# The first modulation slabs shared between VectorE and TensorE, the gain and bias steps spread out, and the last unit split by tile

## The chip, the cores and the metric

The kernel runs on one core of a Trainium2 chip. The metric is the device time of one execution in microseconds, and of the times of several executions the median. The core has TensorE (matrix products into PSUM), VectorE, ScalarE and GpSimd, and SyncE, which only issues DMAs. Each engine works off its own instructions in program order and meets the others at semaphores.

## What is computed

Two layers of a decoder trunk, 256 tokens by 2048 features in float32. Each layer has a mixer (8 attention heads and 8 short-convolution groups, one input and one output projection) and an MLP, and each of the two is modulated by a vector that comes from the condition c.

```python
cond = jax.nn.silu(c)
for l in range(DEPTH):
    mod = cond @ w_mod[l] + b_mod[l]
    sh1, sc1, g1, sh2, sc2, g2 = jnp.split(mod[:, None, :], 6, axis=-1)
    u = x * (1.0 + sc1) + sh1
    proj = u @ w_in[l]
    ...                                   # attention and convolution -> mixed
    x = _layer_norm(DEEPNORM_ALPHA * x + (1.0 + g1) * (mixed @ w_out[l]), ln1_g[l], ln1_b[l])
    u = x * (1.0 + sc2) + sh2
    ff = jnp.square(jax.nn.relu(u @ w_ff1[l])) @ w_ff2[l]
    x = _layer_norm(DEEPNORM_ALPHA * x + (1.0 + g2) * ff, ln2_g[l], ln2_b[l])
```

## The kernel before

**Products.** Every large product is split into high and low parts: an activation is `hi` + `lo`, a weight is `w_hi` + `w_lo`, and three products of 128x512 (L1249 to L1251, in `half` L1263 to L1265) stand for one. The work is cut into *units* (one block of 512 output columns, 16 chunks of the inner dimension) and a unit into 8 *groups* of two chunks: 12 matmuls each, six for either tile of 128 tokens. A layer has 16 mixer units and 32 MLP units. A group's weights (512 KB) come by a DMA from SyncE into one of 4 `raw` buffers. ScalarE copies them to `w_hi` (L455), VectorE makes `w_lo` = raw - w_hi (L755), four groups ahead of their use. A position `p` = 8u + j is group j of unit u, and every engine does its side work of a position beside that group (`side`). The order is written out by hand, through tables of positions.

**Modulation.** `w_mod` is cut into 24 slabs of 1024 columns, and a slab into 16 chunks of 128x1024 (512 KB each). VectorE forms `mod_acc` = sum of chunk k times cond[k] (L766 for the first chunk, L770 for the others, one instruction each). Then TensorE sums `mod_acc` over the partitions with eight 128x1 products against ones (L1325; each shows as two records, so a sum is x16), and VectorE adds the bias. GpSimd issues the chunks' DMAs when a buffer is free.

**The head.** The first four slabs (`START_SLABS`) hold the shift and scale of the first mixer. Slab q gives what four chunks of x need, so the first three units (24 groups) run in four *quarters* of six groups: `start_fill(q)` turns x (L1350, four transposes, twice) and sums slab q between the two; ScalarE applies scale and shift; VectorE makes the low part; six groups follow, and VectorE works on slab q+1 meanwhile. `start_raw` holds 8 chunks. SyncE first loads nine small tensors with one semaphore (`small_in`, the condition is the eighth), and all engines wait for all nine.

**Fills.** Between two sub-layers, x is normalised and turned again (`last_unit`, then `first_unit`). There are three such *fills*. In `first_unit` ScalarE applies scale and shift to each turned tile (L496, four pieces), makes the high part (L500), and VectorE the low part (L828). VectorE's `gain` then multiplies x by the layer norm's g and adds b (L877, L880, two instructions each) for four column blocks, in groups 4 to 7 of that unit. The next step of VectorE in the second layer is the rotary step (`rotate`, L1083 on) at position 7, for the turned q at `Q_AT` = 10.

**The last unit** before a fill does its first four groups for both tiles, then the halves for tile 0 of groups 4 to 7, then the halves for tile 1, so that tile 0 can be finished early. The sum of slab 9 stands among those halves (position 124) in the first mixer. At the very end ScalarE normalises four blocks for each tile, and VectorE's `gain` multiplies and adds for each block.

## Time and profile before

| | |
|---|---|
| median of 3 runs | 2389.97 us (2387.24 to 2394.49) |
| the profiled execution | 2390.11 us |
| its span, first to last instruction | 2388.4 us |
| TensorE busy | 2270.1 us (95%) |
| VectorE busy | 1728.5 us (72%) |
| ScalarE busy | 1115.9 us (47%) |
| chain that ended last | TensorE 84%, VectorE 8%, DMA 3%, issue 3%, ScalarE 2% |
| mean granted clock of TensorE | 0.983 |

The time outside the span is 1.7 us. The page's part 5 groups instructions by line: busy time, mean of one, and the idle time before them with what ended it. A busy TensorE overstates its work where matmuls overlap, so starts of successive matmuls are read from the timeline instead. Where the trace has no clock record (before the first one), the column prints 1.00.

### The profile page before, as it was taken

Reading aid. Unit: us, or ns where it says so; the run is one execution under the profiler, and the core shown is the slowest. Engines: PE = TensorE matmul, PEld = TensorE weight load, DVE = VectorE, ACT = ScalarE, POOL = GpSimd, SP = SyncE. Lnnn points to the kernel's source line nnn. Section 1 sums busy time; section 2 is a strip of 40 time slices with the busy share of each in tenths; the row PEclk is TensorE's granted clock in tenths of the full one; section 3 lists DMA queues with packets and bytes.
Section 4 is the critical chain, followed back from the end, with each engine's and each line's share of the span. In section 5 each row is a group of like instructions: output and inputs, shape, how many; then the busy total and the mean of one; then the engine's idle time right before and its main releaser. Section 6 shows DMA issues by size and latency. Waiting matters only on the chain.

```text
span 2388.4 us, 30251 instructions
## 1 busy us (share of the span) xinstructions
PE 2270.1 (95%) x10384; PEld 1881.5 (79%) x10384; DVE 1728.5 (72%) x1913; ACT 1115.9 (47%) x1424; POOL 227.3 (10%) x400
## 2 busy tenths in 40 slices
PE   3689999989999999999998999999999999999997
PEld 2577888778888888888877888887888888888885
DVE  6898888868777767667878877877766555555566
ACT  2235543356435435435454554435643543543543
POOL 2211111110101101000010100101000000000000
PEclk9789999989999999999999999999999999999998
DMA  9987988958888888887965777886677666666563
GB/s 354 390 289 283 306 324 316 325 211 283 285 283 293 287 276 298 276 276 268 321 242 184 267 262 257 287 293 220 224 237 242 206 213 215 213 205 193 177 228 123
DMA packets 174733, 623.14 MB, mean 261 GB/s; under 512 B 19728, under 2 KB 20496, under 8 KB 174096
## 3 DMA queue, kind: packets, MB, share of 16 engines
q1 hardware_dynamic: 114128, 407.50, 49.8%
q0 software_dynamic: 55296, 201.35, 24.8%
...
## 4 chain that ended last, share of the span: by engine, by line
PE 84%; DVE 8%; DMA 3%; issue 3%; ACT 2%; ACTq 0%; SPq 0%; DVEq 0%; POOLq 0%
PE bank L1249 25%; PE bank L1251 25%; PE bank L1250 25%; DVE mod_acc L770 3%; PE bank L1350 2%; PE bank L1325 2%; DVE w_lo L755 1%; DMA raw<-w_out_dram 1%; DMA Z<-w_mod_dram 1%; ACT w_hi L455 1%; PE bank L1263 1%; PE bank L1264 1%; PE bank L1265 1%; ACT utmp L496 0%; DVE xt L877 0%
## 5 line engine op out<-in xcount | busy, mean ns | idle before, releaser
L755 DVE TENSOR_TENSOR w_lo<-raw,w_hi 128x1024 fp32r<-128x1024 f32 x768 | 937.8, 1224 | 563.7 <-ACT w_hi L455 561.7
L455 ACT ACTIVATE w_hi<-raw 128x1024 fp32r<-128x1024 f32 x768 | 812.4, 1059 | 1129.2 <-PE bank L1251 988.4
L1249 PE MATMUL bank<-w_hi,u_hi 128*128 128x512 f32 x1744 | 695.3, 399 | 0.3 <-DVE u_lo L813 0.3
L1251 PE MATMUL bank<-w_lo,u_hi 128*128 128x512 f32 x1744 | 682.0, 391 | 0.0
L1250 PE MATMUL bank<-w_hi,u_lo 128*128 128x512 f32 x1744 | 681.5, 391 | 0.0
L1249 PE MATMUL bank<-w_hi,m_hi 128*128 128x512 f32 x1216 | 476.9, 392 | 2.8 <-DVE m_lo L813 2.6
L1251 PE MATMUL bank<-w_lo,m_hi 128*128 128x512 f32 x1216 | 474.5, 390 | 0.0
L1250 PE MATMUL bank<-w_hi,m_lo 128*128 128x512 f32 x1216 | 474.3, 390 | 0.0
L770 DVE SCALAR_TENSOR_TENSOR mod_acc<-mod_raw,cond,mod_acc 128x1024 f32<-128x1024 f32 x300 | 383.7, 1279 | 0.6 <-DMA mod_raw<-w_mod_dram 0.6
L1251 PEld LDWEIGHTS bank<-w_lo,u_hi 128*128 128x128 f32 x1744 | 328.9, 189 | 70.0
L1249 PEld LDWEIGHTS bank<-w_hi,u_hi 128*128 128x128 f32 x1744 | 329.5, 189 | 68.6 <-issue 1.4
L1250 PEld LDWEIGHTS bank<-w_hi,u_lo 128*128 128x128 f32 x1744 | 329.5, 189 | 67.3 <-issue 1.4
L435 POOL DMA_DIRECT2D mod_raw<-w_mod_dram x316 | 167.0, 528 | 1745.6 <-DVE mod_acc L770 1521.0
L1249 PEld LDWEIGHTS bank<-w_hi,m_hi 128*128 128x128 f32 x1216 | 229.1, 188 | 51.3 <-DVE m_lo L813 3.4
L1251 PEld LDWEIGHTS bank<-w_lo,m_hi 128*128 128x128 f32 x1216 | 228.9, 188 | 48.0
L1250 PEld LDWEIGHTS bank<-w_hi,m_lo 128*128 128x128 f32 x1216 | 229.0, 188 | 47.0 <-issue 0.2
L1325 PE MATMUL bank<-ones,mod_acc 128*128 128x1 f32 x256 | 38.1, 279 | 50.2 <-DVE mod_acc L770 50.2
L770 DVE SCALAR_TENSOR_TENSOR mod_acc<-Z,cond,mod_acc 128x1024 f32<-128x1024 f32 x60 | 76.9, 1282 | 6.0 <-DMA Z<-w_mod_dram 2.3
L1325 PEld LDWEIGHTS bank<-ones,mod_acc 128*128 128x128 f32 x256 | 38.7, 235 | 52.8 <-issue 30.3
L1350 PE MATMUL bank<-idn,Z 128*128 128x128 f32 x416 | 55.0, 276 | 6.6 <-DVE gate L808 5.4
L1350 PEld LDWEIGHTS bank<-idn,Z 128*128 128x128 f32 x416 | 49.0, 142 | 14.2 <-issue 6.1
L813 DVE TENSOR_TENSOR m_lo<-utmp,m_hi 128x512 fp32r<-128x512 f32 x72 | 49.4, 692 | 14.6 <-ACT m_hi L479 14.6
(128 smaller groups left out, 1116.5 us busy)
## 6 DMA issues: line engine op xcount, KB each, us to landing
raw<-w_ff_dram SPq DMA_DIRECT2D x512, 512.0 KB, 4.2
...
```

Source lines behind the costliest of these rows:

```text
L435: pool.dma_start(mod_raw[:, k:k + 1, :], chunk(r * MODS + (first + k))).then_inc(mod_in[k], 16)
L455: nc.scalar.activation(w_hi[:, j % AHEAD, :], raw[:, j % RAW, :], ACT.Copy).then_inc(hi_ready, 1)
L755: nc.vector.tensor_tensor(w_lo[:, j % AHEAD, :], raw[:, j % RAW, :], w_hi[:, j % AHEAD, :].bitcast(F32), ALU.subtract).then_inc(lo_ready, 1)
L770: ins = nc.vector.scalar_tensor_tensor(out=a, in0=src, scalar=cond[:, k:k + 1], in1=a, op0=ALU.mult, op1=ALU.add)
L813: nc.vector.tensor_tensor(lo[:, chunk:chunk + 2, :], src, hi[:, chunk:chunk + 2, :].bitcast(F32), ALU.subtract).then_inc(split_ready, 1)
L1249: nc.tensor.matmul(o, hi[:, k, tok], wh, start=(k == 0), stop=False)
L1250: nc.tensor.matmul(o, lo[:, k, tok], wh, start=False, stop=False)
L1251: ins = nc.tensor.matmul(o, hi[:, k, tok], wl, start=False, stop=(k == KC - 1))
L1263: nc.tensor.matmul(o[:], hi[:, k, tok], wh, start=(k == 0), stop=False)
L1264: nc.tensor.matmul(o[:], lo[:, k, tok], wh, start=False, stop=False)
L1325: ins = nc.tensor.matmul(b[:, c:c + 1], mod_acc[:, par, c * P:(c + 1) * P], ones[:, 0:1], start=True, stop=True)
L1350: ins = nc.tensor.transpose(b[:, c * SEQ + t * P:c * SEQ + (t + 1) * P], src(c, t), idn[:])
```

## The change

- **Condition first.** SyncE loads c, then the identity and the modulation bias, then the first part of x, then the six other small tensors. The semaphores are separate, so the first steps wait for c alone.
- **Odd chunks on TensorE.** In the four head slabs VectorE multiplies the even chunks only. TensorE multiplies each odd chunk itself (`start_chunk`: eight 128x1 products with the chunk as the stationary operand), accumulating in PSUM bank 5, and the slab's sum is added into the same bank. Bank 4 serves the head's transposes. For slab 0 all eight odd chunks stand ahead of the first turn; for slabs 1 to 3 two chunks stand behind each of the first four groups of the quarter.
- **Gain and bias steps.** They leave groups 4 to 7 of `first_unit` for positions 9, 11, 13, 17 (mixer; MLP: 9, 12, 14, 17). In the second layer `Q_AT` goes from 10 to 14, and waits are added on ScalarE where a buffer is shared with g and b. The modulation chunks of positions 8 to 15 go to later ones.
- **Fills.** VectorE applies scale and shift to two of four pieces of tiles 4 to 7 (`affine`); ScalarE waits for that and does the other two. In `last_unit` the side work of group 7 moves behind tile 1's first half, VectorE finishes tile 0 first, and slab 9's sum goes there, to position 127.
- **The very last unit** runs all eight groups for tile 0, then all for tile 1. Its first four groups' weights lie in `u_hi` and `u_lo`. VectorE alone normalises with two instructions for each block (`centre`, `scaled`).

```diff
-Q_AT = [[22, 34], [10, 34]]
+Q_AT = [[22, 34], [14, 34]]
...
-RED_NOT_BEFORE = {16: MIXER_AT[1] + 8, 17: MIXER_AT[1] + 12}
+RED_NOT_BEFORE = {9: MIXER_AT[0] + 8 * U_MIX - 1, 16: MIXER_AT[1] + 8, 17: MIXER_AT[1] + 12}
...
+GAIN_ORDER = {1: (0, 1, 2, 3), 2: (2, 0, 1, 3), 3: (0, 1, 2, 3)}
+MIX_GAIN_AT = (9, 11, 13, 17)
+FF_GAIN_AT = (8 + 1, 8 + 4, 8 + 6, 16 + 1)
...
-                    + [8 * u + 1 for u in (1, 2, 3, 4, 9, 10, 11, 12, 13)])
+    mixer1 = sorted([8 * u + j for u in range(2, 15) for j in (0, 2, 4, 6)]
+                    + [8 * u + 1 for u in range(2, 14)])
+    ff1 = sorted([8 * w + 4 for w in range(3, 25)] + [8 * w + 1 for w in range(3, 13)])
...
+        def weights(w, ex, unit, j):
+            if unit == FINAL and j < EARLY:
+                return ex[:].rearrange("p k n -> p (k n)")[:, j * GW:(j + 1) * GW]
+            return w[:, j % AHEAD, :]
...
-            small = [(idn[:], ident), (cs[:], cos), (sn[:], sin), (msk[:], mask), (mod_b[:], b_mod),
-                     (mixg[:], mix_g), (cw[:], conv_w), (cc_in[:], cond_c), (lnc[:], ln_cols)]
-            for dst, src in small:
-                sp.dma_start(dst, src).then_inc(small_in, 16)
+            sp.dma_start(cc_in[:], cond_c).then_inc(c_in, 16)
+            sp.dma_start(idn[:], ident).then_inc(first_in, 16)
+            sp.dma_start(mod_b[:], b_mod).then_inc(first_in, 16)
...
             load_x(0)
+            small = [(cs[:], cos), (sn[:], sin), (msk[:], mask), (mixg[:], mix_g), (cw[:], conv_w), (lnc[:], ln_cols)]
+            for dst, src in small:
+                sp.dma_start(dst, src).then_inc(small_in, 16)
...
-                    pool.wait_ge(mod_used, 8 * r + (k - 7))
+                    if k % 2:
+                        pool.wait_ge(chunk_used, 4 * r + ((k - 1) // 2 - 3))
+                    else:
+                        pool.wait_ge(mod_used, 4 * r + (k // 2 - 3))
...
-                    act.wait_ge(pair_used, 8 * unit + (j - AHEAD + 1))
-                nc.scalar.activation(w_hi[:, j % AHEAD, :], raw[:, j % RAW, :], ACT.Copy).then_inc(hi_ready, 1)
+                    act.wait_ge(pair_used, 8 * unit + (j - AHEAD + 1 if unit < FINAL or j < EARLY else j - GROUPS + 1))
+                nc.scalar.activation(weights(w_hi, u_hi, unit, j), raw[:, j % RAW, :], ACT.Copy).then_inc(hi_ready, 1)
...
+                act.wait_ge(turn_done, i + 1)
+                if i >= 2:
+                    act.wait_ge(split_ready, i - 1)
+                for c in range(2):
+                    k = 2 * i + c
+                    ins = nc.scalar.activation(utmp[:, i % 2, c * SEQ:(c + 1) * SEQ], tb[0][:, c * SEQ:(c + 1) * SEQ],
+                                               ACT.Identity, bias=u_shift[:, k:k + 1], scale=u_scale[:, k:k + 1])
+                ins.then_inc(turn_read, 1)
+                act.wait_ge(turn_read, i + 1)
+                nc.scalar.activation(u_hi[:, 2 * i:2 * i + 2, :], utmp[:, i % 2, :], ACT.Copy).then_inc(split_hi, 1)
...
+                if i >= 4:
+                    act.wait_ge(aff_ready, 4 * (fill - 1) + i - 3)
+                for c in range(4 if i < 4 else 2):
...
-            act.wait_ge(small_in, 16 * 9)
+            act.wait_ge(c_in, 16)
             act.wait_ge(ones_ready, 3)
             nc.scalar.activation(cc_e[:], cc_in[:], ACT.Exp, scale=-1.0).then_inc(cond_exp, 1)
+            prepare(0, 0, first=True)
+            prepare(0, 1, first=True)
+            start_fill(0)
+            prepare(0, 2, first=True)
+            prepare(0, 3, first=True)
+            act.wait_ge(small_in, 16 * 6)
...
-                for s in range(4):
-                    normalise(fill, t, s)
...
+            def affine(fill, i):
+                t, s = NORM_ORDER[i]
+                job, n = JOB[("fill", fill)] + i, fill_split(fill, i)
+                wait_job(dve, job)
+                dve.wait_ge(split_ready, n - 1)
+                for c in range(2, 4):
+                    k = 4 * s + c
+                    ins = nc.vector.tensor_scalar(utmp[:, n % 2, c * P:(c + 1) * P], tb[job % 2][:, c * P:(c + 1) * P],
+                                                  u_scale[:, k:k + 1], u_shift[:, k:k + 1], ALU.mult, ALU.add)
+                ins.then_inc(aff_ready, 1)
...
+            def centre(t):
+                for s in range(4):
+                    dve.wait_ge(gb_in[s], 32 * 2 * DEPTH)
+                    sl = xt[:, t, s * NCOL:(s + 1) * NCOL]
+                    nc.vector.scalar_tensor_tensor(out=sl, in0=sl, scalar=mv[:, t, 0:1], in1=lngb[:, s, 0, :],
+                                                   op0=ALU.subtract, op1=ALU.mult)
+            def scaled(t):
+                for s in range(4):
+                    sl = xt[:, t, s * NCOL:(s + 1) * NCOL]
+                    nc.vector.scalar_tensor_tensor(out=sl, in0=sl, scalar=rst[:, t:t + 1], in1=lngb[:, s, 1, :],
+                                                   op0=ALU.mult, op1=ALU.add).then_inc(x_ready, 1)
...
-                for j in range(EARLY, GROUPS):
+                for j in range(EARLY, GROUPS - 1):
                     side(j)
+                last_tile(fill, unit, alpha, 0)
+                side(GROUPS - 1)
                 modulation(fill)
-                last_tile(fill, unit, alpha, 0)
...
+                    if j < 4:
+                        affine(fill, 4 + j)
                     ahead(unit, j)
...
-                        gain(fill, j - 4)
...
+            def start_mod(n, i):
+                k = 2 * i
+                q = n * KC + k
+                mod_step(n, k, n % 2, start_raw[:, q % 8, :], start_in[q % 8], (q // 2, 16 * (q // 8 + 1)))
...
-                one(0)
+                        mod_next(2 * i)
+                        mod_next(2 * i + 1)
                 start_scale(q)
-                one(1)
+                some(0)
                 start_low(2 * q)
-                one(2)
+                some(1)
                 start_low(2 * q + 1)
-                one(3)
...
+                    if layer and p in MIX_GAIN_AT:
+                        gain(2 * layer, MIX_GAIN_AT.index(p))
...
-                                if i < 4:
-                                    start_mods(q + 1, 4 + 3 * i, 3)
+                                start_mod(q + 1, 2 + i)
...
-            start_mods(0, 0, KC)
+            for i in range(KC // 2):
+                start_mod(0, i)
+            dve.wait_ge(first_in, 16 * 2)
...
-            fill, unit = 2 * DEPTH, DEPTH * U_LAYER - 1
-            last_tile(fill, unit, 1.0, 0)
-            last_root(fill, 0)
-            gain(fill, 0, (0,))
-            last_tile(fill, unit, 1.0, 1)
-            gain(fill, 1, (0,))
-            last_root(fill, 1)
-            gain(fill, 2, (0,))
-            gain(fill, 3, (0,))
-            for s in range(4):
-                gain(fill, s, (1,))
+            for t in range(T):
+                last_tile(2 * DEPTH, FINAL, 1.0, t)
+                centre(t)
+                sync(root(norm_index(2 * DEPTH, t), slice(t, t + 1)))
+                scaled(t)
...
+                both = 0 if unit == FINAL else EARLY
+                for j in range(both):
                     group(8 * unit + j, j % AHEAD, GK * j, pacc[par], hi, lo)
                     side(j)
-                for j in range(EARLY, GROUPS):
-                    ins = half(8 * unit + j, j % AHEAD, GK * j, pacc[par][0], 0, hi, lo)
+                for j in range(both, GROUPS):
+                    ins = half(unit, j, pacc[par][0], 0, hi, lo)
                     if j == GROUPS - 1:
                         ins.then_inc(half_done, 1)
-                    side(j)
-                for j in range(EARLY, GROUPS):
-                    half(8 * unit + j, j % AHEAD, GK * j, pacc[par][1], 1, hi, lo).then_inc(pair_used, 1)
+                    else:
+                        side(j)
+                for j in range(both, GROUPS):
+                    half(unit, j, pacc[par][1], 1, hi, lo).then_inc(pair_used, 1)
+                    if j == EARLY:
+                        side(GROUPS - 1)
...
+            def start_chunk(n, i):
+                k = 2 * i + 1
+                q = n * KC + k
+                if n == 0 and i == 0:
+                    pe.wait_ge(cond_ready, 1)
+                if n and i == 0:
+                    pe.wait_ge(sum_read, n)
+                pe.wait_ge(start_in[q % 8], 16 * (q // 8 + 1))
+                for c in range(SC):
+                    ins = nc.tensor.matmul(tb[1][:, c:c + 1], start_raw[:, q % 8, c * P:(c + 1) * P], cond[:, k:k + 1],
+                                           start=(i == 0 and c == 0), stop=False)
+                ins.then_inc(chunk_used, 1)
+            def start_sum(n):
+                pe.wait_ge(mod_used, KC // 2 * (n + 1))
+                for c in range(SC):
+                    ins = nc.tensor.matmul(tb[1][:, c:c + 1], mod_acc[:, n % 2, c * P:(c + 1) * P], ones[:, 0:1],
+                                           start=False, stop=(c == SC - 1))
+                ins.then_inc(sum_done, 1)
...
+                start_turn(2 * q)
+                start_sum(q)
+                start_turn(2 * q + 1)
             def start_units(side):
+                for i in range(KC // 2):
+                    start_chunk(0, i)
...
+                    if q + 1 < START_SLABS and i < START_LABELS - 2:
+                        start_chunk(q + 1, 2 * i)
+                        start_chunk(q + 1, 2 * i + 1)
                     if q + 1 < START_SLABS and i == START_LABELS - 2:
                         start_fill(q + 1)
+                pe.wait_ge(turn_read, 2 * START_SLABS)
+                pe.wait_ge(sum_read, START_SLABS)
```

**TensorE in the head.** Before, from the start of the program; L1350 turns x, L1325 is the sum, L1249 to L1251 the products:

```order
L1350 MATMUL bank<-idn,xt 128x128 x4
L1325 MATMUL bank<-ones,mod_acc 128x1 x8
L1350 MATMUL bank<-idn,xt 128x128 x4
L1249 MATMUL bank<-w_hi,u_hi 128x512
L1250 MATMUL bank<-w_hi,u_lo 128x512
L1251 MATMUL bank<-w_lo,u_hi 128x512
```

After, the same place (L1430 is an odd chunk's product with cond, L1448 the turn, L1438 the sum):

```order
L1430 MATMUL bank<-cond,Z 128x1 x64
L1448 MATMUL bank<-idn,xt 128x128 x4
L1438 MATMUL bank<-ones,mod_acc 128x1 x8
L1448 MATMUL bank<-idn,xt 128x128 x4
L1311 MATMUL bank<-w_hi,u_hi 128x512
L1312 MATMUL bank<-w_hi,u_lo 128x512
L1313 MATMUL bank<-w_lo,u_hi 128x512
```

Sixty-four 128x1 products, eight odd chunks, now stand ahead of the first turn. And after, at the end of the first group and the start of the second, where before the products follow on one another:

```order
L1311 MATMUL bank<-w_hi,u_hi 128x512
L1312 MATMUL bank<-w_hi,u_lo 128x512
L1313 MATMUL bank<-w_lo,u_hi 128x512
L1430 MATMUL bank<-cond,Z 128x1 x16
L1311 MATMUL bank<-w_hi,u_hi 128x512
L1312 MATMUL bank<-w_hi,u_lo 128x512
L1313 MATMUL bank<-w_lo,u_hi 128x512
```

Two chunks (x16) stand between two groups.

**VectorE in the head**, second quarter. Before (L770 a chunk, L755 the low part of weights):

```order
L755 TENSOR_TENSOR w_lo<-raw,w_hi 128x1024 x2
L770 SCALAR_TENSOR_TENSOR mod_acc<-Z,cond,mod_acc 128x1024 x3
L755 TENSOR_TENSOR w_lo<-raw,w_hi 128x1024
L770 SCALAR_TENSOR_TENSOR mod_acc<-Z,cond,mod_acc 128x1024 x3
L755 TENSOR_TENSOR w_lo<-raw,w_hi 128x1024
L770 SCALAR_TENSOR_TENSOR mod_acc<-Z,cond,mod_acc 128x1024 x3
L755 TENSOR_TENSOR w_lo<-raw,w_hi 128x1024
L770 SCALAR_TENSOR_TENSOR mod_acc<-Z,cond,mod_acc 128x1024 x3
```

After (L802 a chunk, L787 the low part):

```order
L787 TENSOR_TENSOR w_lo<-raw,w_hi 128x1024 x2
L802 SCALAR_TENSOR_TENSOR mod_acc<-Z,cond,mod_acc 128x1024
L787 TENSOR_TENSOR w_lo<-raw,w_hi 128x1024
L802 SCALAR_TENSOR_TENSOR mod_acc<-Z,cond,mod_acc 128x1024
L787 TENSOR_TENSOR w_lo<-raw,w_hi 128x1024
L802 SCALAR_TENSOR_TENSOR mod_acc<-Z,cond,mod_acc 128x1024
L787 TENSOR_TENSOR w_lo<-raw,w_hi 128x1024
L802 SCALAR_TENSOR_TENSOR mod_acc<-Z,cond,mod_acc 128x1024
```

One chunk stands where three did.

**VectorE in the first unit of the second layer.** Before (L877 and L880 gain and bias, L1083 the rotary step):

```order
L755 TENSOR_TENSOR w_lo<-raw,w_hi 128x1024
L877 TENSOR_TENSOR xt<-xt,Z 128x512 x2
L880 TENSOR_TENSOR xt<-xt,Z 128x512 x2
L755 TENSOR_TENSOR w_lo<-raw,w_hi 128x1024
L877 TENSOR_TENSOR xt<-xt,Z 128x512 x2
L880 TENSOR_TENSOR xt<-xt,Z 128x512 x2
L1083 TENSOR_TENSOR Z<-bank,cs 128x4x64 x2
```

After (L921 and L924 gain and bias, L1148 to L1159 the rotary step):

```order
L787 TENSOR_TENSOR w_lo<-raw,w_hi 128x1024 x4
L1148 TENSOR_TENSOR Z<-bank,cs 128x4x64 x2
L1149 TENSOR_TENSOR Z<-bank,nsn 128x4x64
L1150 TENSOR_TENSOR Z<-bank,sn 128x4x64
L1159 TENSOR_TENSOR Z<-Z 128x512
L1148 TENSOR_TENSOR Z<-bank,cs 128x4x64 x2
L1149 TENSOR_TENSOR Z<-bank,nsn 128x4x64
```

The rotary step no longer has the gains ahead of it; they come behind it.

## Rows read from the trace of the kernel before

**Rows 1.** Stretches of the head; columns: busy of each engine, clock, DMA share, GB/s.
```profile
0.00:46.50 46.50, 5.78 (x25) 4.92 (x25) 26.02 (x31) 7.81 (x11) 13.99 (x30) 1.00 0.90 340
46.50:78.00 31.50, 20.20 (x85) 17.25 (x86) 28.79 (x28) 8.37 (x11) 8.32 (x16) 0.81 1.03 407
```

**Rows 2.** Timeline of the opening: start us, us, engine, line, work, [idle before <-releaser].
```profile
15.32 0.22 ACT L729 ACTIVATE cc_e<-cc_in 128x16 f32<-128x16 f32 x1 [12.89 <-DMA lnc<-ln_cols_dram]
...
17.43 16.57 DVE L770 SCALAR_TENSOR_TENSOR mod_acc<-Z,cond,mod_acc 128x1024 f32<-128x1024 f32 x12
...
17.53 1.09 PE L1350 MATMUL bank<-idn,xt 128*128 128x128 f32 x4 [17.53 <-DMA xt<-x_dram]
...
39.94 3.58 PE L1325 MATMUL bank<-ones,mod_acc 128*128 128x1 f32 x16 [21.32 <-DVE mod_acc L770]
...
46.50 0.80 PE L1249 MATMUL bank<-w_hi,u_hi 128*128 128x512 f32 x1 [0.28 <-DVE u_lo L813]
```

**Rows 3.** Timeline of TensorE in the second quarter, and where the last begins.
```profile
71.73 3.55 PE L1325 MATMUL bank<-ones,mod_acc 128*128 128x1 f32 x16 [9.71 <-DVE mod_acc L770]
...
86.93 0.39 PE L1249 MATMUL bank<-w_hi,u_hi 128*128 128x512 f32 x1
...
89.65 0.39 PE L1249 MATMUL bank<-w_hi,u_hi 128*128 128x512 f32 x1
...
142.25 0.78 PE L1249 MATMUL bank<-w_hi,u_hi 128*128 128x512 f32 x1
```

**Rows 4.** Timeline of TensorE around a slab sum in a dense stretch.
```profile
316.14 1.84 PE L1325 MATMUL bank<-ones,mod_acc 128*128 128x1 f32 x16
317.84 0.49 PE L1249 MATMUL bank<-w_hi,u_hi 128*128 128x512 f32 x1
```

**Rows 5.** Stretches by granted clock, columns as in rows 1.
```profile
103.50:107.10 3.60, 3.55 (x16) 3.47 (x16) 2.80 (x4) 0.00 (x0) 0.68 (x2) 0.50 1.02 409
407.50:414.20 6.70, 6.70 (x21) 5.54 (x21) 5.45 (x9) 0.94 (x2) 1.05 (x2) 0.50 0.76 276
404.10:407.40 3.30, 2.16 (x15) 1.62 (x14) 1.09 (x2) 2.12 (x3) 0.53 (x1) 1.00 1.01 402
489.40:499.60 10.20, 9.49 (x30) 8.20 (x31) 2.30 (x6) 0.00 (x0) 0.53 (x1) 0.50 0.77 262
509.90:513.20 3.30, 3.30 (x9) 2.57 (x8) 3.23 (x7) 2.96 (x5) 2.72 (x1) 0.50 0.50 144
1238.20:1257.00 18.80, 13.95 (x74) 10.75 (x73) 13.43 (x22) 16.53 (x36) 6.88 (x4) 1.00 0.56 196
1284.70:1288.10 3.40, 3.02 (x12) 2.77 (x13) 3.40 (x5) 1.20 (x2) 0.11 (x1) 0.50 0.67 170
```

**Rows 6.** Timeline of TensorE, last unit of the first mixer and fill 1.
```profile
490.11 3.54 PE L1325 MATMUL bank<-ones,mod_acc 128*128 128x1 f32 x16 [2.87 <-DVE mod_acc L770]
...
509.63 0.56 PE L1263 MATMUL bank<-w_hi,u_hi 128*128 128x512 f32 x1 [2.60 <-issue]
```

**Rows 7.** Timeline of TensorE, first unit of the second layer (fill 2).
```profile
1253.68 0.63 PE L1382 MATMUL bank<-idn,xt 128*128 128x128 f32 x4 [0.86 <-ACT utmp L496]
...
1256.69 0.63 PE L1382 MATMUL bank<-idn,xt 128*128 128x128 f32 x4 [0.99 <-ACT utmp L496]
...
1285.08 1.94 PE L1350 MATMUL bank<-idn,Z 128*128 128x128 f32 x8 [5.44 <-DVE gate L808]
```

**Rows 8.** Timeline of the tail, TensorE's last product, then VectorE.
```profile
2370.91 0.39 PE L1265 MATMUL bank<-w_lo,m_hi 128*128 128x512 f32 x1
```

**Rows 9.** Timeline of the tail, VectorE.
```profile
2355.84 2.36 DVE L755 TENSOR_TENSOR w_lo<-raw,w_hi 128x1024 fp32r<-128x1024 f32 x2
...
2372.03 0.69 DVE L892 TENSOR_TENSOR bank<-bank,gate 128x512 f32<-128x512 f32 x1
...
2374.50 0.15 DVE L902 TENSOR_SCALAR ve<-mv 128x1 f32<-128x1 f32 x1
...
2384.14 0.69 DVE L880 TENSOR_TENSOR xt<-xt,Z 128x512 f32<-128x512 f32 x1
```

121 lines of the change are left out of this document (60 added, 61 removed).

## The prediction

> **What bounds the kernel now.** The table first: TensorE is busy in 95% of the span and holds 84% of the chain that ended last. So the questions are where TensorE waits, where it runs at half clock, and what the change adds to it. The stretches and TensorE's timeline answer them. In the opening nothing starts until the small tensors are in: ScalarE's first step comes at 15.3, VectorE then multiplies chunks at 1.38 us each, the first slab sum starts at 39.94 and the first product at 46.50 [rows 2]. In the second quarter TensorE idles 9.7 us for VectorE's chunks, sums slab 1 at half clock (3.55 us), and the last quarter's first products start at 142.25 [rows 3]. From 46.50 to 142.25 are 95.75 us, three quarters of 31.9 us. That looks like a VectorE bound, but the DMA column stands at 1.03 with 407 GB/s [rows 1]. A quarter needs 16 chunks, six groups of weights and a part of x, 23 x 0.524 MB = 12.1 MB, and that takes 29.6 us at this rate. A quarter can gain 2.3 us at most, whatever VectorE does.
>
> **The opening.** With c loaded first, the wait of 12.89 us [rows 2] goes, and data is late next. The first odd chunk is the second of 512 KB. At 340 GB/s [rows 1], with x between and some 3 us until the first bytes, I put it at 7.4 us (bounds 5 and 10). Eight odd chunks on TensorE cost what a slab sum costs, since shape, type and count are the same (eight 128x1 products, x16 records): 3.58 us in this part of the program [rows 2]. 7.4 + 8 x 3.58 = 36.0. VectorE's eight even chunks take 8 x 1.38 = 11 us and hide. Then the turn, 1.1 us, which before was done early (at 17.53) and now stands behind the chunks, the sum, 3.6, and the way from the sum's end to the first product, 46.50 - 43.52 = 3.0 [rows 2]. The first product starts at **43.7** against 46.5. If TensorE took the chunks at full clock the data would set the pace: 16 chunks, four weights and a part of x are 11 MB, 30 us, and the first product comes at 38.
>
> **The three quarters.** VectorE loses 8 x 1.38 = 11 us a quarter, and TensorE gets eight chunks. A group is 89.65 - 86.93 = 2.72 us [rows 3]. A sum in a dense stretch costs 1.70 us from its start to the next product's start, and 0.14 more in the first product behind it, 1.84 in all [rows 4]; so a pair of chunks costs 1.84 + 1.70 = 3.54. The turns and the sum between groups: 1.84 plus the 3.0 from above, 4.8. At full clock a quarter is 6 x 2.72 + 4 x 3.54 + 4.8 = 16.3 + 14.2 + 4.8 = **35.3 us**, over the 31.9 of before and over the 29.6 of the DMA. The idle time that VectorE caused is filled with more work than it was long. This is the bound from below: 3 x 35.3 = 105.9, 10.2 us more than before.
>
> Now the clock. What holds it up? In 103.50:107.10 TensorE is busy 3.55 of 3.60 us with nothing but 128x1 products, and the clock is 0.50 and stays there until wide products have run [rows 5]. In 404.10:407.40 it is busy 2.16 of 3.30 us, about half of that in 128x1 products, and from 407.50 on the clock is 0.50 for 6.7 us [rows 5]. In 1238.20:1257.00 it is idle for a quarter of the time but works in wide products and turns, and keeps 1.00 [rows 5]. In these rows 128x1 products did not hold the clock up. The new quarter has four stretches of 3.5 us and one of 4.8 us without a wide product. Stretches of that length without one, behind work at full clock, are few: in 404.10:407.40 and on, and at the starts of the fills, where two turns and the wait for the first tile make 3.6 us. The clock fell in the first, and at fill 1 (509.90), but not at fill 2 (1238.20) [rows 5, 6]. A single sum of 1.8 us in dense work never lowered it. I take four falls a quarter. A fall lasts 3.3 us (509.90), 6.7 us (407.50) or 10.2 us (489.40) [rows 5], and half of it is lost, 1.7 to 5.1 us. I take 2.5, between the first two, because every pair of chunks is followed by a group of wide products that can raise the clock again: 10 us a quarter. Ends of the range: nothing, and half clock throughout, where a quarter doubles to about 68 us. So a quarter is 45.3 us, three are 135.9, and the last quarter's products start at 43.7 + 135.9 = 179.6 against 142.25: **+37.4 us**. TensorE is the bound behind it, so nothing of this is given back.
>
> The Trainium skill, "TensorE: Matmul & The Clock Gate", section "Why this matters for your kernels", tells to avoid idle gaps between bursts of matmuls and to keep TensorE busy continuously, and gives idle time as what lowers the clock. By that advice the chunks in the old 9.7 us gap are good for the clock, and the result is the second case below. The row of 103.50:107.10 does not agree: busy, and at 0.50.
>
> **The sum of slab 9.** TensorE waits 2.87 us for VectorE at 490.11 [rows 6] and then runs 10.2 us at 0.50 [rows 5], 5.1 lost. It is moved three halves of tile 0 and one of tile 1 later, 4 x 1.36 = 5.4 us, more than the wait. VectorE's chunks before it stay. The fill's scale needs the sum, but tile 0's mean and variance are being made at that time. **-8.0 us** (0 to -8).
>
> **Gain and bias, and q.** TensorE waits 5.44 us for q at 1285.08 [rows 7], and the clock is 0.50 for 3.4 us behind it [rows 5]. VectorE had four gains ahead of the rotary step, each four instructions of 0.69 that overlap a little [rows 9], 2.6 us. Now the step stands ahead of them and q is turned four positions later, 11 us. The wait and 1.7 us of half clock go: **-7.1 us** (0 to -7.1). The moved gains and chunks lie in units in which VectorE has 2.72 us a group for 1.2 (low part) and at most one 1.3 or 2.6; I cost them at nothing. If that cover is missing, they show as waits for `w_lo`.
>
> **Fills.** TensorE waits 0.86 and 0.99 us for ScalarE's four pieces [rows 7], three fills, 5.6 us in all. Half of the pieces go to VectorE, but ScalarE waits for them, one more hand-over each. I take **-3 us** (-5.6 to +2). The 2.60 us wait at 509.63 [rows 6] is one tile's way through three engines with all four pieces still on ScalarE, and stays.
>
> **Tail.** The last product starts at 2370.91 [rows 8], and the end is at 2388.4. The last unit starts 96 x 0.2265 = 21.7 us earlier, at 2349.4. With halves first, group 4's low weights are needed 4 x 1.36 us later, at 2354.8, but VectorE makes them behind the last residual, from 2355.84 on, and one takes half of 2.36 [rows 9]: 2357.0: TensorE waits **+2.2 us**. Tile 0 is finished and stored under tile 1's products. Tile 1 needs, after its last product, at 2373.5: the step from L892 to L902, 2374.65 - 2372.03 = 2.6; four `centre` at some 0.65 = 2.6; the root, five steps as small as L902, at 0.2 = 1.0; four `scaled` 2.6; and the last store as before, 2388.4 - 2384.83 = 3.6 [rows 9]. 2373.5 + 12.4 = 2385.9, **-2.5 us** in all.
>
> **Sum.** Against the profiled execution, 2390.11 (span 2388.4 and 1.7 around it; the median of the runs is 2389.97, so one stands for the other): +37.4 - 8.0 - 7.1 - 3 - 2.5 = +16.8, **2406.9 us**.
>
> **The rivals.** Second case, not slower: *the chunk products keep the clock that wide products raised*. It decides at 1.00 in the quarters. The opening stays at 43.7, the quarters take 105.9, products of the last start at 149.6, +7.3; with -20.6 from the rest, 2376.8. For it: at 1238.2 a stretch as long did not lower the clock. Against: the two rows of 128x1 work. Chance 0.18. With the opening at full clock as well, 2371, 0.04. Third: *falls are shorter or rarer*, 5 us a quarter in place of 10: 2391.9, chance 0.12. Fourth: *the savings do not come*, because VectorE's moved gains, the hand-over in the fills and the last unit's low weights only change which wait is last (the -7.1, -3 and -2.5 gone): 2419.5, chance 0.12. Fifth: *half clock throughout the quarters*: 43.7 + 3 x 68 = 248, +105 - 20.6 = 2475, chance 0.04; the group of 5.1 us at half clock between two pairs speaks against it, as wide products of 5 to 7 us raised the clock each time. My forecast has 0.50.
>
> **How the numbers follow.** About 0.3% (7.2 us) can be told from no change here. Faster (under 2382.8): second case, 0.22. Same: third case and the edge of the forecast, 0.15. Slower: the rest, 0.63. The range leaves out the fifth case, the full opening and some of the edges: 2374 to 2424. The forecast's own range is 2396 to 2418.
>
> **What would show it.** The new line of 128x1 products with 3.5 us for two at 0.50 and 1.8 and 1.7 at 1.00; first wide product near 43.7; TensorE without idle in the quarters and VectorE idle for some 11 us in each; clock under 0.8 from 44 to 180; the last quarter's products at 180. No wait at slab 9's sum nor at the turn of q; a wait of 2 us for low weights in the last unit. If the last quarter's products start before 150, the clock step is wrong; if a chunk costs under 1.2 us, the price from the sum's row is.

## The result and the profile after

The changed kernel takes 2430.52 us (median of 4 runs, 2428.29 to 2433.19) against 2390.91: ratio 1.0167, 95% interval 1.015 to 1.0184. The profiled execution is the one of 2428.29 us, with a span of 2426.6. I had forecast 2406.9 and a range of 2374 to 2424: slower was right, the size was not, +38.2 us in the span where I had +16.8.

The busy line, the line of the clock (40 slices; a 9 is 0.9 or more) and the group of the new 128x1 products, from the page after:

```profile
PE 2364.4 (97%) x10896; PEld 1969.8 (81%) x10896; DVE 1695.3 (70%) x1903; ACT 1101.5 (45%) x1392; POOL 227.3 (9%) x400
PEclk9678999999999999999999999999999999999998
L1430 PE MATMUL bank<-cond,Z 128*128 128x1 f32 x512 | 77.3, 285 | 11.1 <-DMA Z<-w_mod_dram 11.1
```

TensorE is busier than before (97%), and the kernel is slower. The 32 chunks cost it 77.3 us of busy time, and the clock is below 0.9 in slices 2 to 4. The stretches of the opening, of the three quarters and of what follows answer to [rows 1, 5]. The columns are the stretch and its length in us, the busy time and count of TensorE's products, its weight loads, VectorE, ScalarE and GpSimd, then the granted clock, the DMA share and GB/s:

```profile
0.00:46.20 46.20, 33.21 (x153) 32.49 (x153) 14.56 (x22) 5.52 (x8) 13.48 (x29) 1.00 0.97 372
46.20:93.40 47.20, 42.39 (x213) 37.69 (x213) 18.59 (x20) 10.42 (x14) 8.44 (x16) 0.75 0.78 283
93.40:143.50 50.10, 45.29 (x226) 39.38 (x225) 18.12 (x20) 9.64 (x12) 8.44 (x16) 0.74 0.64 221
143.50:195.80 52.30, 47.49 (x227) 41.65 (x225) 19.21 (x20) 9.64 (x12) 6.30 (x12) 0.70 0.52 190
195.80:540.00 344.20, 337.48 (x1593) 279.77 (x1592) 302.70 (x380) 157.84 (x239) 49.08 (x93) 0.99 0.88 310
```

A quarter takes 47 to 52 us in place of 31.9. The DMA, which bounded it before (1.03), falls to 0.52, so it is TensorE that bounds it now. (The 1.00 of the first row is no sign of full clock: the products in it take 3.5 us, as at 0.50. The column has no record there.) ScalarE's first step and TensorE's timeline at the marks (start us, us, what, count, idle before it and what ended it):

```profile
2.67 0.21 ACT L760 ACTIVATE cc_e<-cc_in 128x16 f32<-128x16 f32 x1 [0.23 <-DMA cc_in<-c_dram]
7.55 3.54 PE L1430 MATMUL bank<-cond,Z 128*128 128x1 f32 x16 [7.55 <-DMA Z<-w_mod_dram]
30.94 3.57 PE L1430 MATMUL bank<-cond,Z 128*128 128x1 f32 x16 [2.07 <-DMA Z<-w_mod_dram]
46.18 0.79 PE L1311 MATMUL bank<-w_hi,u_hi 128*128 128x512 f32 x1 [0.27 <-DVE u_lo L845]
87.46 3.57 PE L1438 MATMUL bank<-ones,mod_acc 128*128 128x1 f32 x16 [3.22 <-DVE mod_acc L802]
195.77 0.78 PE L1311 MATMUL bank<-w_hi,u_hi 128*128 128x512 f32 x1
546.55 1.84 PE L1391 MATMUL bank<-ones,mod_acc 128*128 128x1 f32 x16
571.51 0.63 PE L1486 MATMUL bank<-idn,xt 128*128 128x128 f32 x4 [0.93 <-ACT utmp L522]
2397.04 0.53 PE L1325 MATMUL bank<-w_hi,m_hi 128*128 128x512 f32 x1 [2.14 <-DVE w_lo L787]
2414.90 0.39 PE L1327 MATMUL bank<-w_lo,m_hi 128*128 128x512 f32 x1
```

The opening gained almost nothing (46.18 against 46.50). The last quarter's products start at 195.77 against 142.25 [rows 3], +53.5 us. Slab 9's sum (546.55) has no wait, where it had one of 2.87 [rows 6]. The last product starts at 2414.90 against 2370.91 [rows 8], +44.0. So the savings behind the quarters came, and the quarters ate them.

An idle time that I had not foreseen stands before the sum at 87.46 (3.22 us), and again at 139.23 and 189.84. VectorE's timeline just ahead of it:

```profile
84.98 1.23 DVE L787 TENSOR_TENSOR w_lo<-raw,w_hi 128x1024 fp32r<-128x1024 f32 x1 [7.10 <-ACT w_hi L472]
86.12 1.28 DVE L802 SCALAR_TENSOR_TENSOR mod_acc<-Z,cond,mod_acc 128x1024 f32<-128x1024 f32 x1
91.06 0.17 DVE L1007 TENSOR_TENSOR mod_col<-bank,mod_b 128x8 f32<-128x8 f32 x1 [3.66 <-PE bank L1438]
```

VectorE has 7 us to spare and its last chunk is there to take. But in its program the step stands behind a low part of weights. That waits for `w_hi`, and ScalarE makes `w_hi` only when TensorE is through with the group that used the same buffer (83.89, 8.47 us idle for it), which is the last one ahead of the sum. So the last chunk step can't begin before the quarter's products are done, and the sum waits for it.

### The profile page after: what moved, and what is told of

Read it like the earlier page. It is cut to its first block, busy times and chain, and to the rows that moved or that the text cites. A ratio compares the mean times of both kernels' runs of the same rounds, so it can differ in the third digit from the quotient of the medians.

```text
span 2426.6 us, 31262 instructions
## 1 busy us (share of the span) xinstructions
PE 2364.4 (97%) x10896; PEld 1969.8 (81%) x10896; DVE 1695.3 (70%) x1903; ACT 1101.5 (45%) x1392; POOL 227.3 (9%) x400
## 4 chain that ended last, share of the span: by engine, by line
PE 92%; DVE 4%; issue 1%; DMA 1%; ACT 1%; ACTq 0%; POOL 0%; DVEq 0%; POOLq 0%; SPq 0%
PE bank L1311 27%; PE bank L1313 27%; PE bank L1312 27%; PE bank L1430 3%; PE bank L1416 2%; PE bank L1325 1%; PE bank L1326 1%; PE bank L1327 1%; DVE mod_acc L802 1%; DMA Z<-w_mod_dram 1%; PE bank L1391 1%; ACT w_hi L472 1%; DVE w_lo L787 1%; PE bank L1438 1%; PE bank L1400 0%
## 5 line engine op out<-in xcount | busy, mean ns | idle before, releaser
L787 DVE TENSOR_TENSOR w_lo<-raw,w_hi 128x1024 fp32r<-128x1024 f32 x764 | 933.2, 1224 | 624.9 <-ACT w_hi L472 622.6
L1311 PE MATMUL bank<-w_hi,u_hi 128*128 128x512 f32 x1744 | 705.9, 405 | 0.3 <-DVE u_lo L845 0.3
L1313 PE MATMUL bank<-w_lo,u_hi 128*128 128x512 f32 x1744 | 690.3, 396 | 0.0
L1312 PE MATMUL bank<-w_hi,u_lo 128*128 128x512 f32 x1744 | 690.2, 396 | 0.0
L1313 PE MATMUL bank<-w_lo,m_hi 128*128 128x512 f32 x1200 | 468.7, 391 | 0.0
L1312 PE MATMUL bank<-w_hi,m_lo 128*128 128x512 f32 x1200 | 468.5, 390 | 0.0
L1311 PEld LDWEIGHTS bank<-w_hi,u_hi 128*128 128x128 f32 x1744 | 335.2, 192 | 69.3 <-issue 1.4
L1312 PEld LDWEIGHTS bank<-w_hi,u_lo 128*128 128x128 f32 x1744 | 335.1, 192 | 68.8 <-issue 1.4
L802 DVE SCALAR_TENSOR_TENSOR mod_acc<-mod_raw,cond,mod_acc 128x1024 f32<-128x1024 f32 x300 | 383.6, 1279 | 0.2
L1312 PEld LDWEIGHTS bank<-w_hi,m_lo 128*128 128x128 f32 x1200 | 226.3, 189 | 46.5 <-issue 0.2
L1430 PEld LDWEIGHTS bank<-cond,Z 128*128 128x128 f32 x512 | 78.7, 243 | 12.7 <-issue 7.5
L1430 PE MATMUL bank<-cond,Z 128*128 128x1 f32 x512 | 77.3, 285 | 11.1 <-DMA Z<-w_mod_dram 11.1
L1416 PE MATMUL bank<-idn,Z 128*128 128x128 f32 x416 | 54.1, 273 | 1.2 <-DVE Z L1159 1.1
L802 DVE SCALAR_TENSOR_TENSOR mod_acc<-Z,cond,mod_acc 128x1024 f32<-128x1024 f32 x28 | 35.8, 1280 | 19.6 <-DMA Z<-w_mod_dram 19.6
```

The source lines that it names most:

```text
L787: nc.vector.tensor_tensor(weights(w_lo, u_lo, unit, j), raw[:, j % RAW, :], weights(w_hi, u_hi, unit, j).bitcast(F32), ALU.subtract).then_ ...
L802: ins = nc.vector.scalar_tensor_tensor(out=a, in0=src, scalar=cond[:, k:k + 1], in1=a, op0=ALU.mult, op1=ALU.add)
L1311: nc.tensor.matmul(o, hi[:, k, tok], wh, start=(k == 0), stop=False)
L1312: nc.tensor.matmul(o, lo[:, k, tok], wh, start=False, stop=False)
L1313: ins = nc.tensor.matmul(o, hi[:, k, tok], wl, start=False, stop=(k == KC - 1))
L1416: ins = nc.tensor.transpose(b[:, c * SEQ + t * P:c * SEQ + (t + 1) * P], src(c, t), idn[:])
```

## The experiments

The theory from here on: the rest of the change is a gain, and the chunk products on TensorE cost some 59 us, by their own time at full clock (14 us a quarter), by half clock that comes with 3.5 us stretches without a wide product, and by VectorE's order ahead of the sums. The rivals: the rest of the change costs too; TensorE's share of narrow work lowers the clock, however it is spread; the chunks' waits and hand-overs cost the time, not the products. All runs are set against runs of the kernel before on the same chip (medians 2388.6 to 2390.8).

**All chunks back on VectorE.**

```diff
-START_SHARE = START_SLABS * KC // 2
+START_SHARE = START_SLABS * KC
 def start_mod(n, i):
-    k = 2 * i
+    k = i
 ...
-    start_chunk(q + 1, 2 * i)
-    start_chunk(q + 1, 2 * i + 1)
```

> The changed kernel with all 64 chunks of the head back on VectorE in the old order; condition first, gains, fills and last unit stay as changed. Theory A (the chunk products on TensorE are the whole loss, the rest of the change is a gain): the opening is paced by data, 16 chunks, and the first product comes near 38; the quarters take 31.9 us as before, so the last quarter's products start near 134, 62 us ahead of the changed kernel's 195.8: about 2367 us. Rival B (the rest of the change costs too, or the head's new banks and waits do): the last quarter's products start later than 140 or the end lies above 2385.

Measured: 2371.42 us (2369.07 to 2372.81), ratio 0.9916 (0.9899 to 0.9932). That is 59 us under the changed kernel and 19 under the one before. Its sums and first products, from TensorE's timeline:

```profile
36.10 3.57 PE L1440 MATMUL bank<-ones,mod_acc 128*128 128x1 f32 x16 [24.48 <-DVE mod_acc L799]
42.66 0.80 PE L1311 MATMUL bank<-w_hi,u_hi 128*128 128x512 f32 x1 [0.28 <-DVE u_lo L842]
133.15 3.54 PE L1440 MATMUL bank<-ones,mod_acc 128*128 128x1 f32 x16 [7.82 <-DVE mod_acc L799]
139.05 0.77 PE L1311 MATMUL bank<-w_hi,u_hi 128*128 128x512 f32 x1
```

Two of its quarters, from the view of stretches:

```profile
42.70:74.60 31.90, 20.15 (x85) 17.16 (x86) 28.91 (x29) 10.57 (x15) 8.48 (x16) 0.80 1.03 408
74.60:107.10 32.50, 23.14 (x97) 19.35 (x95) 27.48 (x28) 9.54 (x12) 8.01 (x16) 0.76 1.00 387
```

The clock is hardly higher here (0.80, 0.76) than in the changed kernel. But TensorE is idle for a third of the quarter, and the data sets the pace (1.03, 1.00), so little hangs on it. The head without TensorE's chunks, with the condition loaded first, brings the first product 3.8 us forward (42.66 against 46.50), not the 8.5 us that I had expected: VectorE waits for the data of most chunks, and starts on the last one at 34.76. The run ends 4 us later than the 2367 of theory A for that reason. The rest of the change is a gain, as forecast.

**VectorE's chunk steps earlier in the quarter.** Two steps in the first group of a quarter and one in each of the next, so that none is left for the last.

```diff
-start_mod(q + 1, 2 + i)
+for s in ((2, 3), (4,), (5,), (6,), (7,), ())[i]:
+    start_mod(q + 1, s)
```

> The changed kernel with VectorE's last even chunk of each slab one group earlier, ahead of the low part that waits for the group just run. Theory A (the 3.4 us idle before the sums of slabs 1 to 3 is this order on VectorE): the idle goes, 10 us, and up to 5 us of half clock with it: 2413 to 2421 us. Rival B (the sum waits for data, or the idle only stands in for something as late): 2428 to 2431 us, the idle stays with another releaser.

Measured: 2417.26 us (2414.06 to 2418.61), ratio 1.0109 (1.0092 to 1.0126), 13 us under the changed kernel, as expected. TensorE's timeline at the sum and the first product of the next quarter:

```profile
83.31 1.84 PE L1439 MATMUL bank<-ones,mod_acc 128*128 128x1 f32 x16
87.68 0.78 PE L1312 MATMUL bank<-w_hi,u_hi 128*128 128x512 f32 x1
```

Its three quarters, from the view of stretches:

```profile
45.70:87.70 42.00, 40.20 (x213) 35.70 (x213) 18.76 (x20) 10.49 (x14) 8.44 (x16) 0.77 0.86 318
87.70:135.10 47.40, 45.65 (x227) 39.97 (x225) 18.09 (x20) 9.65 (x12) 8.44 (x16) 0.72 0.68 244
135.10:182.60 47.50, 45.75 (x226) 39.84 (x225) 19.03 (x20) 9.65 (x12) 6.30 (x12) 0.72 0.55 198
```

The idle time before the sum is gone, and the sum, in dense work now, runs at full clock (1.84 for 3.57). It was VectorE's order that made it. The quarters are 42.0, 47.4 and 47.5 us, 45.6 in the mean.

**The same chunks, spread.** As the last run, but of the two chunks behind a group one is moved into the middle of the group, so that no stretch without a wide product is longer than 1.7 us, the quarter's turn and sum aside. Same work, same share.

```diff
 for kk in range(GK):
+    if kk == 1 and mid is not None:
+        mid()                        # start_chunk(q + 1, 2 * i)
     k = k0 + kk
```

> The second kernel of this set (last chunk early) with the same eight chunks a slab on TensorE, but one in the middle of each of the four groups and one behind it, so no stretch without a wide product is over 1.8 us, except at the turns. Theory A (the length of the stretches lowers the clock): the clock holds 1.00 but for the turns, a quarter takes 36 to 39 us in place of 46 to 47, about 2385 to 2395 us. Rival B (the share of 128x1 work counts, whatever its pieces): the same time as the second kernel within 5 us.

Measured: 2387.52 us (2383.21 to 2395.96, 10 runs), ratio 0.9991 (0.9977 to 1.0004), 30 us under the last run. A chunk in its timeline, 1.84 us between wide products:

```profile
51.87 1.84 PE L1433 MATMUL bank<-cond,Z 128*128 128x1 f32 x16
```

Its three quarters, and a stretch behind a turn:

```profile
45.70:80.30 34.60, 32.84 (x213) 29.62 (x213) 18.69 (x20) 10.43 (x14) 8.40 (x16) 0.99 0.97 372
80.30:117.00 36.70, 34.95 (x227) 31.44 (x225) 18.11 (x19) 9.45 (x12) 8.16 (x17) 0.96 0.84 316
117.00:153.90 36.90, 35.15 (x226) 31.54 (x224) 18.78 (x20) 9.59 (x13) 6.23 (x13) 0.95 0.71 266
...
80.30:83.10 2.80, 2.80 (x9) 2.22 (x8) 2.53 (x3) 1.65 (x3) 0.04 (x1) 0.50 0.90 351
```

The clock falls only at the turns, 3.4 us each time, and a quarter is 36.1 us in the mean. Set the two runs side by side: the clock lacks 0.23, 0.28 and 0.28 of the three quarters there, 9.7 + 13.3 + 13.3 = 36 us, and 0.3 + 1.5 + 1.8 = 4 us here; the quarters differ by 136.9 - 108.3 = 28.6 us, so the clock accounts for all of it and comes out some 4 us high. In the code nothing but the order of TensorE's products differs. So it is the arrangement that lowers the clock here, and the rival by share falls.

**A quarter of the chunks on TensorE.** From the changed kernel: only every fourth chunk goes to TensorE, one behind a group; VectorE takes 12 of 16.

```diff
-    k = 2 * i + 1
+    k = 4 * i + 3
 ...
-    start_chunk(q + 1, 2 * i)
-    start_chunk(q + 1, 2 * i + 1)
+    start_chunk(q + 1, i)
```

> The changed kernel with only every fourth chunk on TensorE (four a slab, one behind each of the first four groups), twelve on VectorE, all of them ahead of the group's wait. Theory A: TensorE has 16.3 + 4 x 1.84 + 4.8 = 28.5 us a quarter at full clock, VectorE 12 x 1.38 + 7.3 + 2 = 26, the DMA 29.6, so a quarter takes 30 to 31.5 us at the DMA's pace, the clock stays high, the first product comes near 38 and the last quarter's near 131: 2360 to 2367 us. Rival B (VectorE's chain of chunk, low part and sum binds all the same, or the clock falls in single chunks too): a quarter of 33 us or more, over 2372 us.

Measured: 2386.64 us (2381.15 to 2390.09, 10 runs), ratio 0.9978 (0.9966 to 0.9989). Theory A was 20 us too low, and the numbers are those of rival B: quarters of 34.4, 37.8 and 38.4 us. The first product stands at 45.66, not near 38, since the opening's last chunk comes to TensorE only at 34.95. One of the last quarter's chunks in TensorE's timeline:

```profile
143.42 2.72 PE L1431 MATMUL bank<-cond,Z 128*128 128x1 f32 x12 [5.07 <-DMA Z<-w_mod_dram]
```

The last quarter, and the stretch of that wait:

```profile
117.90:156.30 38.40, 31.57 (x162) 27.35 (x161) 24.15 (x24) 9.65 (x12) 6.32 (x13) 0.81 0.69 248
137.90:143.40 5.50, 0.45 (x2) 0.03 (x1) 4.59 (x4) 1.06 (x1) 0.00 (x0) 0.74 1.03 416
```

GpSimd's timeline in that quarter:

```profile
126.19 0.53 POOL L428 DMA_DIRECT2D Z<-w_mod_dram  x1 [5.31 <-DVE mod_acc L802]
```

TensorE runs into its chunk before the data is there: 5.07 us here, 2.14 and 3.78 in the two quarters before. The transfers of the quarter use 0.69 of the DMA and 1.03 just then. GpSimd issues them in one order into eight buffers, and had waited 5.31 us for VectorE to free one. That the waits come from this coupling of the two readers is read from these rows; other buffers weren't tried. What is shown is the cost: TensorE works in program order, and a late chunk now stops the wide products behind it.

The clock fell too, at the waits and the turns, and once at neither. In the first quarter a single chunk (69.19, 1.95 us) stands between wide products, TensorE has no gap, and this follows:

```profile
68.90:72.30 3.40, 3.40 (x24) 2.90 (x23) 1.91 (x2) 1.06 (x1) 0.00 (x0) 1.00 1.03 412
72.30:75.70 3.40, 3.40 (x11) 2.62 (x10) 1.79 (x2) 0.23 (x1) 1.31 (x3) 0.50 1.04 388
```

So single chunks don't always keep the clock: in the third run's trace none of 24 was followed by a fall, here one was. Why this one isn't shown.

**One of eight products.** From the second run, with TensorE doing one of a chunk's eight products; the kernel leaves out the other seven, so the modulation lacks most of the odd chunks.

```diff
-for c in range(SC):
+for c in range(1):
     ins = nc.tensor.matmul(tb[1][:, c:c + 1], start_raw
```

> As the second run (chunk steps early), but TensorE does one of the eight 128x1 products of every odd chunk; seven eighths of the odd chunks' column sums are left out of the modulation. Transfers, waits and VectorE's work are as in that run (2417.3 us, quarters 45.75, 87.68, 135.06, 182.60). Theory (the quarters are long because of the products themselves and the half clock that their stretches bring): a quarter's work is 16.3 for groups, 4.8 for turn and sum and 4 x 0.4 for what is left of the pairs, 22.7 us, which is under what the data takes, so the DMA bounds: quarters of 29 to 32 us, first product at 38 to 42, last quarter's products at 125 to 138, 2360 to 2370 us. Rival (waits and hand-overs of the chunks cost the time, not the products): quarters stay over 40 us and the whole over 2400.

Measured: 2377.27 us (2374.49 to 2381.65), ratio 0.9948 (0.9932 to 0.9964). One of its chunks in TensorE's timeline:

```profile
58.72 0.59 PE L1431 MATMUL bank<-cond,Z 128*128 128x1 f32 x2 [4.00 <-DMA Z<-w_mod_dram]
```

Its first two quarters, from the view of stretches:

```profile
42.00:78.40 36.40, 27.17 (x102) 22.17 (x103) 19.42 (x21) 10.72 (x15) 8.45 (x16) 0.79 1.03 408
78.40:113.20 34.80, 27.21 (x114) 22.37 (x113) 18.07 (x20) 9.64 (x13) 8.44 (x16) 0.79 0.85 330
```

The second run's order of steps had saved 13 of the 59 us, and without the products 40 more are gone, so the rival by waits and hand-overs falls as the main cause. These 40 hold both the products' own time and the half clock; the third run puts 30 on the arrangement. But I had expected 2360 to 2370. A quarter stays at 34 to 36 us, longer than the 32.1 with all chunks on VectorE, since TensorE waits for chunk data here as in the run before. In the first quarter the DMA is full (1.03), in the second it isn't (0.85). In the second run, with all eight products, TensorE has no wait for a chunk in the quarters: its longer work covers them.

**The fills' pieces back on ScalarE.** From here on the base is the first run (2371.42).

```diff
-if i >= 4:
-    act.wait_ge(aff_ready, 4 * (fill - 1) + i - 3)
-for c in range(4 if i < 4 else 2):
+for c in range(4):
```

> The fastest kernel so far (all chunks on VectorE, the rest as changed; 2371.4 us) with the fills' pieces of the operand all on ScalarE again. My forecast gave the split over two engines 3 us in three fills. The traces show waits of 1.3 and 0.3 us in a fill's first unit against 1.0 and 1.2 before, so some 0.5 us each: 2371 to 2374 us, and TensorE waits of about 1 us twice in each fill. If the split were worth what I had said, 2374.5.

Measured: 2373.85 us (2370.21 to 2375.99), ratio 0.9928 (0.9909 to 0.9947). TensorE's wait for the first late piece in fill 1, from its timeline:

```profile
513.33 0.63 PE L1478 MATMUL bank<-idn,xt 128*128 128x128 f32 x4 [0.86 <-ACT utmp L516]
```

The same piece in the changed kernel:

```profile
568.56 0.63 PE L1486 MATMUL bank<-idn,xt 128*128 128x128 f32 x4 [0.16 <-ACT utmp L522]
```

0.86 in place of 0.16, and the second wait about as long in both: the split is worth 0.7 us a fill, some 2 us in the three, as expected from the traces and not the 3 us of my forecast. The medians alone can't tell it from nothing.

**Slab 9's sum back at its old place.**

```diff
-RED_NOT_BEFORE = {9: MIXER_AT[0] + 8 * U_MIX - 1, 16: ...
+RED_NOT_BEFORE = {16: ...
```

> The same base (2371.4 us) with the sum of slab 9 at its old place. By my forecast TensorE waits 2.9 us for VectorE there again and then runs some 10 us at half clock: +7 to +8 us, 2378.5 to 2379.5. Rival (the wait before came from VectorE being late with chunks, which other parts of the change have cured): no wait at that sum, 2371.

Measured: 2374.28 us (2371.86 to 2375.64), ratio 0.9935 (0.9919 to 0.9952), between the two expectations. The sum in TensorE's timeline (the view ends at 488.0, so it shows 12 of the sum's 16 records):

```profile
486.69 1.47 PE L1391 MATMUL bank<-ones,mod_acc 128*128 128x1 f32 x12 [3.56 <-DVE mod_acc L799]
```

The stretch behind it:

```profile
488.20:495.00 6.80, 6.80 (x19) 5.45 (x19) 0.17 (x1) 0.00 (x0) 0.00 (x0) 0.50 0.76 283
```

The wait and the half clock behind it are back: 3.6 + 3.4 = 7 us at that place. Against the base the medians show only 2.9 us. A likely reason is in the traces: in the base's profiled execution the clock fell for 3.4 us at each of the three fills, and once more at 437 and at 2342. In this one only the first fill's fall is there. So falls at such places come in one execution and not in another, though the code there is the same, 1.7 us each time. The medians don't settle the size; the place in the trace does.

**The last unit's first low weights ahead of a residual.** VectorE makes group 4's ahead of the residual of the unit before.

```diff
+if w < FF_UNITS - 1 or j:
     ahead(base + w, j)
 ...
+if final and w == FF_UNITS - 2:
+    ahead(base + w + 1, 0)
```

> The same base (2371.4 us); VectorE makes the last unit's first low weights (group 4) ahead of the residual of the unit before. Theory: TensorE's wait of 2.3 us at 2338.4 goes, and with it the half clock of 3.4 us behind it (1.7 lost): -4 us, 2367.4. Rival: the residual is late then, or the low weights of group 5 take over the wait: 2369 to 2372.

Measured: 2367.01 us (2365.66 to 2371.32), ratio 0.9907 (0.9888 to 0.9926). The number fits the theory and TensorE's timeline fits the rival:

```profile
2338.74 0.50 PE L1328 MATMUL bank<-w_hi,m_hi 128*128 128x512 f32 x1 [1.91 <-DVE w_lo L784]
```

The stretch around it:

```profile
2338.00:2342.00 4.00, 3.26 (x14) 2.68 (x15) 2.95 (x3) 0.00 (x0) 0.00 (x0) 1.00 0.00 0
```

The wait has moved by one half group and is 1.91 us long, against 2.14. What is gone is the clock's fall behind it.

**The residual behind all four.**

```diff
+if final and w == FF_UNITS - 1:
+    residual(FINAL - 1, (FINAL - 1) % 2, 2, 1.0)
-if 4 <= s and w < FF_UNITS - 1:
+if 4 <= s and w < FF_UNITS - 1 - final:
```

> The fastest base (all chunks on VectorE, the rest as changed; 2371.4 us) with VectorE's residual of the unit before the last moved behind the last unit's four low weights. The run with only the first low weight moved kept a wait of 2.07 us, one half group later: the next one stood behind the residual (1.3 + 1.3 + 1.3 us). Theory: with all four ahead no low weight is late, the wait and the half clock behind it go: 2.3 + 1.7 = 4.0 us, 2367 to 2368. Rival: the last unit's weights arrive too late (ScalarE waits 1.7 us for the last one), 1 us of wait stays: 2369.

Measured: 2366.13 us (2364.26 to 2367.0), ratio 0.9902 (0.9885 to 0.9918). TensorE runs the last unit without a wait, as the same stretch shows:

```profile
2338.00:2342.00 4.00, 4.00 (x19) 3.34 (x18) 3.43 (x5) 0.51 (x1) 0.00 (x0) 1.00 0.00 0
```

This is the fastest kernel of the study: 64 us under the changed one, 22 us under the one before. Its interval overlaps that of its base, so the step itself rests on the trace.

**q turned at its old place.**

```diff
-Q_AT = [[22, 34], [14, 34]]
+Q_AT = [[22, 34], [10, 34]]
```

> The same base (2371.4 us) with q of layer 1's first group of heads turned at its old place, four positions (11 us) earlier; the gains stay where the change puts them. It tells which of the two edits took TensorE's 5.4 us wait away. If the order of VectorE's work did it (rotary step ahead of the gains), there is no wait and the time stays at 2371. If VectorE is late anyway by the 2.6 us of gains that were ahead of it less, 5.4 - 2.6 = 2.8 us of wait stay and perhaps 1.7 of half clock: 2374 to 2376. If only the later place did it: the whole 5.4 + 1.7, 2378.5.

Measured: 2368.67 us (2366.38 to 2372.39), ratio 0.9916 (0.9899 to 0.9932). TensorE's turn of q, the row that answers to [rows 7]:

```profile
1267.78 1.03 PE L1416 MATMUL bank<-idn,Z 128*128 128x128 f32 x8
```

There is no wait, though the turn of q comes 40.5 us behind the fill's first turns (1227.29), where the base has 54.1. So the gains, which no longer stand ahead of VectorE's rotary step, took the 5.44 us away, and moving q wasn't needed.

## Why the prediction was right or wrong

**The opening (forecast 43.7, measured 46.18).** The first chunk at 7.4 (7.55), 3.58 us for each of eight (3.54 to 3.58), all at half clock: right. The step "7.4 + 8 x 3.58" took the data as there. TensorE waits 0.55 + 2.07 + 0.96 = 3.6 us for chunks. I had said that the data sets the pace only at full clock, with a first product at 38. In the runs with fewer products or none on TensorE the last chunk is taken up at 34.2 to 35.0 all the same, and the first product comes at 41.96 at the earliest (one product in eight). So the data alone allows about 42, and at 372 GB/s it was too close to TensorE's own work to be left out.

**The quarters (forecast 45.3, measured 49.9 in the mean; this is the step that failed).** The work itself was sized nearly right. I had 35.3 us with six groups. The first quarter has five, so it is 32.6 there and 35.3 in the others; with the clock held up they took 34.6, 36.7 and 36.9 (third run). The clock's price was about right too: the second run's quarters are 9.4, 12.1 and 12.2 us over these bounds, where I had taken four falls of 2.5 us, 10. In its trace four or five stretches of 3.4 or 6.8 us at 0.50 begin in each quarter. What I left out is VectorE's order. I wrote "TensorE without idle in the quarters", because I had only asked how much VectorE has to do (11 us less) and not where its last chunk step stands: behind a low part that can't be made before TensorE is through with the last group ahead of the sum. 3.2 us of idle three times, and more half clock behind it (the sums of slabs 1 and 3 ran at half clock, that of slab 2 didn't), make the 13 us between the changed kernel and the second run. It was to be read from the order of VectorE's instructions. Opening and quarters together are 53.5 us where I had 37.4.

**The second case (chunk products keep the clock up, 0.18)** fell: 0.75, 0.74 and 0.70 in the quarters. The Trainium skill, "TensorE: Matmul & The Clock Gate", section "Why this matters for your kernels", advises to avoid idle gaps and keep TensorE busy; the numbers here don't follow it. The row at 103.50 that I had held against it was weak, since TensorE had been idle for 7.8 us before it and the clock was low already. In the changed kernel TensorE has no gap from 46.2 to 72.9. A pair of chunks starts at 56.66 and one at 66.17, and the clock falls behind each:

```profile
55.90:59.30 3.40, 3.40 (x30) 3.25 (x28) 1.29 (x2) 1.06 (x1) 0.15 (x1) 0.99 0.99 374
59.30:66.00 6.70, 6.70 (x21) 5.64 (x22) 1.13 (x1) 0.00 (x0) 1.96 (x4) 0.50 1.03 417
66.10:69.40 3.30, 3.30 (x31) 3.26 (x30) 1.88 (x2) 1.06 (x1) 0.53 (x1) 1.00 0.95 381
69.50:72.90 3.40, 3.40 (x10) 2.79 (x10) 0.45 (x1) 0.00 (x0) 1.05 (x2) 0.50 0.89 287
```

The quarter's first pair (50.35) was followed by no fall. The third case (5 us a quarter) fell with the 9 to 12 us of the second run, and the fifth (half clock throughout) with the changed kernel's clocks of 0.70 to 0.75.

**Slab 9 (-8.0).** The start of fill 1 turns moved by 552.48 - 506.00 = 46.5 where the quarters had given 53.5: -7.0, confirmed in place by the seventh run.

**Gain, bias and q (-7.1).** From fill 2's turns (+46.0) to fill 3's (+40.7) it is -5.3, about the wait itself. The half clock that went with it is not seen again, since the clock now falls at fill 2, where it hadn't: that part of the term was not the wait's to give.

**Fills (-3).** Mis-sized: the late pieces cost 0.16 + 0.93 us of wait in a fill after, and 0.86 + 0.99 before [rows 7], so 0.8 us a fill. Fill 2's share stands within the -5.3 above, beside the clock's fall there; the sum below leaves 1.0 us for fills 1 and 3. ScalarE still makes two of four, and the last hand-over remains.

**Last unit and tail (-2.5).** The wait for low weights came as said (2.14, forecast 2.2). I had not priced the half clock behind it, 1.7 us, the stretch:

```profile
2397.40:2400.70 3.30, 3.30 (x9) 2.64 (x8) 2.99 (x3) 0.00 (x0) 0.00 (x0) 0.50 0.00 0
```

From the last product's start to the end it is 11.7 us against 17.5, -5.8; with the +2.1 and +1.7 that is -2.0.

**Sum:** +53.5 - 7.0 - 5.3 - 2.0 = +39.2; the measured +38.2 leaves -1.0 for fills 1 and 3. Of the 21.4 us that I was too low, 13.7 lie in the quarters, 2.5 in the opening, and 5.3 in the savings behind the head (15.3 in place of 20.6). The fourth case, "the savings do not come", is refuted by the first run: without the chunks the change is 19 us faster.
